# A decoder layer with 32 experts on one core: gate/up weights in 4 MB loads with 32 KB packets, one more early slot, and one piece of a LayerNorm moved from ScalarE and GpSimd to VectorE

## The reference: what is computed

```python
x = LN(alpha * x + hybrid_mixer(x))            # 8 FoX heads + 8 MoBA heads
x = LN(alpha * x + memory_cross_attention(x))  # 4 heads, 256 memory tokens
# moe_ffn: top-4 of 32 experts, softmax over the four
logits = xt @ w_router + b_router
top_val, top_idx = lax.top_k(logits, 4); gates = softmax(top_val)
def expert_block(xb, e):
    h = xb @ w_gate_up[e] + b_gate_up[e]       # 1024 -> 2048
    g, u = min(h[:, :1024], 7), clip(h[:, 1024:], -7, 7)
    return ((u + 1) * g * sigmoid(1.702 * g)) @ w_down[e] + b_down[e]
x = LN(alpha * x + sum_k gates_k * expert_k(x))
```

## Time and profile before

| what | us |
|---|---|
| median of the timed runs | 1237.19 |
| the profiled execution's own time | 1236.11 |
| its span in the trace | 1234.2 |
| PE busy, share of the span | 1156.5, 94% |
| PE's waits for gate/up weights in the experts | 42.7 |
| transfers on SP's queue, share of 16 engines' span | 86.0% |

### The profile page before, as it was taken

How to read it: one execution, slowest core, us unless ns; L and a number is a source line. 1 busy time by engine, 2 the same in 40 slices (tenths; PEclk the granted TensorE clock), 3 DMA queues, 4 the chain that set the end, 5 groups by cost and what they waited for, 6 DMA issues and landing times.

```text
span 1234.2 us, 13113 instructions
## 1 busy us (share of the span) xinstructions
PE 1156.5 (94%) x5364; PEld 524.5 (42%) x5364; DVE 219.2 (18%) x548; ACT 134.6 (11%) x289; POOL 51.2 (4%) x61
## 2 busy tenths in 40 slices
PE   8999999998999999989899999998989898999985
PEld 6686746754344343324233434333333333333321
DVE  1132112114121111111112111211111111111113
ACT  2133101222010000000000000000000000000002
POOL 0033003210000000000000000000000000000000
PEclk9999999998999999999999999999999999999998
DMA  9943333375899999999999999999999999999994
GB/s 357 310 153 136 106 133 136 136 270 193 363 397 429 427 428 430 427 429 429 429 428 427 427 427 427 431 427 429 427 427 430 427 430 428 429 428 427 431 427 184
DMA packets 54349, 445.50 MB, mean 361 GB/s; under 512 B 10120, under 2 KB 11280, under 8 KB 29744
## 3 DMA queue, kind: packets, MB, share of 16 engines
q1 hardware_dynamic: 52160, 440.48, 86.0%
q10 hardware_dynamic: 2160, 4.60, 1.1%
HBM read 444.01 MB, written 1.06 MB: 361 GB/s over the span
## 4 chain that ended last, share of the span: by engine, by line
PE 50%; DMA 46%; DVE 2%; issue 1%; ACT 1%; SPq 0%; POOL 0%; DVEq 0%
DMA ring<-in_w_gate_up 45%; PE bank L1482 18%; PE bank L1164 9%; PE bank L1177 9%; PE bank L1505 6%; PE bank L1389 2%; PE bank L1450 1%; PE bank L1465 1%; PE bank L1334 1%; PE bank L1492 0%; PE bank L1237 0%; PE bank L1312 0%; PE bank L1136 0%; PE bank L1250 0%; DMA x_nat<-in_x 0%
## 5 line engine op out<-in xcount | busy, mean ns | idle before, releaser
L1482 PE MATMUL bank<-ring,PT 128*64 128x512 f32 x2016 | 448.9, 596 | 42.8 <-DMA ring<-in_w_gate_up 42.7
L1482 PEld LDWEIGHTS bank<-ring,PT 128*64 128x64 f32 x2016 | 140.9, 137 | 344.9 <-issue 260.5
L1505 PE MATMUL bank<-ring,NCt 128*64 128x512 f32 x1024 | 229.0, 600 | 0.7 <-ACT NCt L715 0.7
L1505 PEld LDWEIGHTS bank<-ring,NCt 128*64 128x64 f32 x1024 | 71.2, 138 | 155.1 <-issue 142.8
L1164 PE MATMUL bank<-reg_bc,ring 128*128 128x256 f32 x512 | 113.7, 381 | 1.8 <-ACT reg_bc L637 1.8
L1062 DVE TENSOR_SCALAR reg_k<-bank 128x512 f32<-128x512 f32 x32 | 22.1, 692 | 473.1 <-PE bank L1482 473.1
L1164 PEld LDWEIGHTS bank<-reg_bc,ring 128*128 128x128 f32 x512 | 96.3, 190 | 18.1 <-issue 5.4
L706 ACT ACTIVATE reg_v<-reg_k 128x512 f32<-128x512 f32 x32 | 20.2, 630 | 751.1 <-DVE reg_k L1062 751.1
L1079 DVE COPY vc<-bank 128x512 f32<-128x512 f32 x32 | 22.1, 692 | 305.6 <-PE bank L1505 305.6
L1389 PEld LDWEIGHTS bank<-L,reg_a 128*128 128x128 f32 x512 | 64.4, 200 | 24.5 <-issue 23.5
L1389 PE MATMUL bank<-L,reg_a 128*128 128x128 f32 x512 | 70.6, 292 | 0.8 <-DVE L L985 0.8
(11 more groups left out here) (204 smaller groups left out, 494.6 us busy)
## 6 DMA issues: line engine op xcount, KB each, us to landing
ring<-in_w_gate_up SPq DMA_DIRECT2D x126, 2048.0 KB, 24.3
ring<-in_w_down SPq DMA_DIRECT2D x64, 2048.0 KB, 20.3
ring<-in_w_in SPq DMA_DIRECT2D x6, 2048.0 KB, 15.5
ring<-in_w_ck SPq DMA_DIRECT2D x2, 2048.0 KB, 20.6
ring<-in_w_cv SPq DMA_DIRECT2D x2, 2048.0 KB, 10.6
ring<-in_w_mix_out SPq DMA_DIRECT2D x2, 2048.0 KB, 7.7
ring<-in_w_cq SPq DMA_DIRECT2D x2, 2048.0 KB, 7.7
ring<-in_w_co SPq DMA_DIRECT2D x2, 2048.0 KB, 9.5
```

The lines of the kernel that those rows point to most:

```text
L1482: last = mm(ps[half * CAP:(half + 1) * CAP, :], xgT[:, k, i * CAP:(i + 1) * CAP], w[:, j, col:col + HALF], start=False, stop=(k == KD - 1) ...
L1505: last = mm(xy_ps[half * CAP:(half + 1) * CAP, :], hT[:, a:a + CAP], w[:, j, half * HALF:(half + 1) * HALF], start=(k == 0), stop=(k == KD ...
```

## The change

- **Slots.** `kcT` and `vc` (keys and values of the cross-attention) lie in a seventh slot of `ring`, index 6. What else lived in them moves into the freed space of `L`, `reg_v`, `reg_k` and the mask constants; the activation is computed in place. Expert 1 so has three slots (`reg_q`, `reg_bc`, ring 6) that can be filled ahead of the experts.
- **Loads.** For experts 2 to 30 the gate/up weights are two loads of 4 MB (ring 3 and 4, ring 5 and 6); each partition's share is one run of 32 KB on both sides. Experts 0, 1 and 31 keep 2 MB gate/up loads. Down weights keep 2 MB loads, in ring 0 and 1 from expert 2 on. In the steady state ring 2 is idle.
- **Waits.** The first 4 MB load of an expert waits until PE has used the first four steps of the expert before, the second until it has used all eight.
- **LayerNorm.** Tile 1's second half of `x2` goes to DVE (`gain2(1)`, `scale_and_bias2(1)`), behind the places of tile 1.
- **Biases.** The clearing of `bdn` waits for the first expert's gate/up products, and ACT loads it after the first pair; `bgu` is loaded without waiting for a clearing.

```diff
-        ring = sb("ring", [P, CH, SLOT])
+        ring = sb("ring", [P, NSLOT, SLOT])          # CH = 6, NSLOT = 7
-        kcT = sb("kcT", [P, KD, NMEM])
-        vc = sb("vc", [P, 2, D])
+        reg_kv = ring[:, NSLOT - 1, :]
+        kcT = reg_kv[:, 0:2048].rearrange("p (k m) -> p k m", k=KD)
+        vc = reg_kv[:, 2048:4096].rearrange("p (t d) -> p t d", t=2)
...
+        def gate_up_source(e, c, rows=slice(0, GUJ)):                     # GUJ = 4
+            w = w_gate_up[0][bass.ds(e, 1), c * GUJ * P:(c + 1) * GUJ * P, :]
+            return w.rearrange("o (p j) n -> p (o j) n", p=P)[:, rows, :]
+        FIRST = [[ring[:, 0, :], ring[:, 1, :]], [ring[:, 2, :], ring[:, 3, :]]]
+        SECOND = [[early_q, early_bc], [ring[:, 6, :], ring[:, 0, :]]]
+        STEADY = [[ring[:, 3, :], ring[:, 4, :]], [ring[:, 5, :], ring[:, 6, :]]]
+        def gate_up_slots(c):
+            return ring[:, 3 + 2 * c:5 + 2 * c, :].rearrange("p a (j n) -> p (a j) n", j=2)
+        def down_slot(c, e):
+            return ring[:, {0: 4, 1: 1}.get(e, 0) + c, :].rearrange("p (j n) -> p j n", j=DNJ)
...
-            with sp.Fori(3, NE) as n:
-                for c in range(CH):
-                    wait_used(c, n)
-                    load_chunk(n, c)
+            def load_expert(e, n):
+                sp.wait_ge(chunks_used, n * 4 - 2)
+                load_gate_up(e, 0)
+                sp.wait_ge(gu_done, n)
+                load_gate_up(e, 1)
+                sp.wait_ge(chunks_used, n * 4)
+                load_down(e, 0)
+                sp.wait_ge(y_done, n)
+                load_down(e, 1)
+            with sp.Fori(3, NE - 1) as n:
+                load_expert(n, n)
...
-            nc.gpsimd.memset(bdn, 0.0).then_inc(moe_zeroed, 1)
-            for n, (tt, half) in enumerate(((0, 0), (0, 1), (1, 1))):
+            for n, (tt, half) in enumerate(((0, 0), (0, 1))):
...
+            pool.wait_ge(gu_done, 1)
+            nc.gpsimd.memset(bdn, 0.0).then_inc(moe_zeroed, 1)
...
-            normalise(1, 1)
...
             places(S, 0, False, (1,)).then_inc(s_ready, 1)
+            gain2(1)
+            scale_and_bias2(1)
...
-                    if j == 0:
-                        pe.wait_ge(chunk_in[c], n * 16 + 16)
+                    if halves and j == 0:
+                        pe.wait_ge(gate_up_half_in[c], halves * 16)
+                    elif j == (2 if halves else 0):
+                        pe.wait_ge(gate_up_in[c], n * 16 + 16)
```

More of the change, by code:

```diff
@@ L257, in hybrid_layer @@
         hT = NCt[:, :, :].rearrange("p a b -> p (a b)")[:, 0:512]
-        bgu = kcT[:, 0:2, :].rearrange("p k m -> p (k m)")
-        bdn = vc[:, 0, :]
+        bgu = after[:, 1536:2048]
+        bdn = after[:, 0:1024]
         memT = reg_c
@@ L325, in hybrid_layer @@
         moe_zeroed = sem("moe_zeroed")
-        chunk_in = [sem(f"chunk_in{c}") for c in range(CH)]
+        gate_up_in = [sem(f"gate_up_in{c}") for c in range(2)]
+        gate_up_half_in = [sem(f"gate_up_half_in{c}") for c in range(2)]
+        down_in = [sem(f"down_in{c}") for c in range(2)]
         chunks_used = sem("chunks_used")
@@ L455, in _ @@
[L455 to L467, removed]
@@ L468, in _, with load_half @@
-            for c in range(CH):
[L469 to L474, removed]
-            with sp.Fori(3, NE) as n:
-                for c in range(CH):
-                    wait_used(c, n)
-                    load_chunk(n, c)
+            def load_half(e, slot, c, half):
+                done = (gate_up_half_in, gate_up_in)[half][c]
+                sp.dma_start(two_rows(slot), gate_up_source(e, c, HALVES[half])).then_inc(done, 16)
@@ new lines, in _ @@
+            with sp.Fori(3, NE - 1) as n:
+                load_expert(n, n)
+            e = NE - 1
+            for c in range(2):
+                for half in range(2):
+                    if (c, half) == (1, 1):
+                        sp.wait_ge(gu_done, e)
+                    else:
+                        sp.wait_ge(chunks_used, e * 4 - 3 + 2 * c + half)
+                    load_half(e, STEADY[c][half], c, half)
+            sp.wait_ge(chunks_used, e * 4)
+            load_down(e, 0)
@@ L1465, in biases, with gate_up @@
                     mm(ps[:, :], bsel[rows, i, :], bgu[rows, :], start=True, stop=False, skip_group_check=True)
-            def gate_up(p, i, first):
+            def gate_up(p, i, first, halves=0):
                 n = p * 2 + i
@@ L1512, in pair @@
             def pair(p, first=False, with_base=False, last=False):
-                gate_up(p, 0, first)
+                gate_up(p, 0, first, 1 if first else 0)
                 if not first:
@@ L1532, in pair @@
                 down(p, 0, range(KD), first)
-                gate_up(p, 1, first)
+                gate_up(p, 1, first, 2 if first else 3 if last else 0)
                 if not last:
```

159 lines of the change are left out of this document (95 added, 64 removed).

## The result

| kernel | median, us | runs | ratio to before, 95% interval |
|---|---|---|---|
| before | 1237.87 | 4 | |
| changed | 1247.06 | 4 | 1.0073 (1.0054 to 1.0092) |

The change makes the kernel slower by 0.7%. The forecast was 1232.0, faster, in a range from 1228.5 to 1238.5. The profiled execution took 1247.79 us, its span is 1246.0.

The account below looks back on a forecast made before the run. The weight transfers were taken to bound the experts, with PE setting the stream's start. Terms +0.65 - 1.15 - 4.7 = -5.2 gave 1230.9 from the profiled 1236.1, or 1232.0 us against the median 1237.2, range 1228.5 to 1238.5.

Parts of the forecast that it names:

- part 4: Expert loop: waiting for whole 4 MB loads costs 0, at most +1 us, with PE's products the same in number and size.
- pair 6: Experts 12 and 13, with extra PE work: the load of expert 14 just in time, X + 36.25 against X + 36.4.
- part 2: End of the router: x2 work moved from POOL to DVE lets PE's last gather begin sooner, -1.15 us.
- part 1: Slots and waits before expert 3: the early chunk buys only an idle gap, expert 3's data begin later, +0.65 us.
- part 3: Gate/up loads of experts 3 to 30: 32 KB packets make each 4 MB load 0.085 us shorter, -4.7 us in all.
- expert 31's last landing: End of the kernel: halves for expert 31 keep this as the bound, so the 28.3 us after it stay.
- rival B: Start of the experts: shorter DVE waits may keep PE's clock high, 2.9 us earlier in all, 1229.1 us; chance 0.08.
- What B priced as the opposite: Expert loop: PE's clock falls behind each longer wait, 3.9 us a pair, less than the slack of 5.0; no time lost.
- Part 3's line through 2 and 16 KB: Packet cost from two measured stretches: 10.6 ns a packet and 27.2 bytes a ns; 431 to 432 GB/s expected in the experts.
- rival D: Expert loads: a packet's own cost is smaller, 3.5 ns, so part 3 is -1.6 us, total 1235.1; chance 0.10.
- rival A: Expert loads: 32 KB packets are no faster, 16 KB is already the plateau, total 1236.7 us; chance 0.20.
- rival C: Expert loads: the longer runs are read more slowly, +3.7 us at 0.075 a load, up to 1273.7 us; chance 0.10.

Follow-up runs that it names:

- experiment 2: The kernel before, with its gather reading x2 four columns apart instead of two (wrong columns); 1244.99 us, ratio 1.0062.
- experiment 1: The changed kernel, with its gather reading x2 two columns apart instead of four (wrong columns); 1231.43 us, ratio 0.9950.
- experiment 7: The changed kernel's slots, with every gate/up load 2 MB in 16 KB packets with its own wait, and gather distance two; 1230.20 us, ratio 0.9952.
- experiment 5: The kernel before, with the four products of each gather reading x2 every 3rd, 5th, 6th and 8th float (wrong columns); 1240.84 us, timed once.
- experiment 8: The changed kernel, 4 MB loads with 32 KB packets, with x2 stored in pairs so the gather reads every 2nd float and right columns; 1232.26 us, ratio 0.9961.
- experiment 3: The changed kernel, with 4 MB loads as two runs of 16 KB a partition, so gather distance two is right; 1234.85 us, ratio 0.9975.
- experiment 6: The kernel before, with only tile 1's second half of x2 moved to VectorE; 1233.38 us, ratio 0.9966.
- experiment 9: The kernel of experiment 8, with gate/up loads of experts 2, 3, 12 to 15 and 31 in 2 MB halves with a wait each; 1228.51 us, ratio 0.9927.
- experiment 4: The changed kernel, with x2 stored so a gather reads 128 neighbouring floats, LayerNorm 4 apart and the base step 128 apart; 1237.63 us, ratio 0.9998.

## Why the prediction was wrong

**The step that failed** is in part 4: "PE's products are the same in number and size". They are, and it does not follow that they cost the same. I counted `GUJ` as the number of rows in a load and did not follow it into the gather, where it is the distance between the floats that PE reads. So the sum has no term for it. Experiment 2 gives its price on the kernel before, 7.0 us, experiment 1 its price in the changed one, 15.6. Of 57.9 us of PE's work most lies in the waits for weights, but the stream's start is PE's, and the slack of a pair falls from 5.0 to 0.9 us, so that pair 6 breaks the stream for 5.5 us instead of 0 to 1.

The traces show where the larger price in the changed kernel comes from; by their spans it is 14.9 against 8.5 us. Nearly all of the difference is the start: expert 2 is 10.9 us late there and 5.0 in experiment 2. The start loses the high clock that part 2 had won (1.8 us in expert 0's products, where experiment 2's are 0.8 us quicker than before), and the gathers ahead of expert 0 delay its products by 4.8 us instead of 1.7. Another 2.0 us come at the end: with 4 MB hand-overs PE waits for no weights after expert 29's second load, so slow gathers count there, while the kernels of experiments 2 and 7 still wait for their last loads. Pair 6 costs less there than in experiment 2, 1.9 against 3.1.

The Trainium skill ("SBUF — State Buffer", section "Door 1: The DMA port swizzle (why `[64,N]` ≈ `[32,N]`)") names lines of 16 bytes and wants "≥2 hits per line". This rule, which speaks against the change, I had not weighed, and experiments 2, 5 and 8 agree with it: 196 ns with two floats in each 16 bytes, 328 with one. Its next sentence, that 4 fp32 is how far one can stride for free, does not agree: at a distance of 4 the load is slow.

**The other terms,** each from kernels that differ in little else:

| term | forecast | measured | from |
|---|---|---|---|
| parts 1 and 4, slots and 4 MB waits | +0.65 to +1.65 | +1.5 | experiments 3 and 6: 1234.85 - 1233.38 |
| part 2, end of the router | -1.15 | -4.2 | experiment 6: 1233.38 - 1237.58 |
| part 3, 32 KB packets | -4.7 | -3.4, -2.6 | experiments 1 and 8 less 3 |
| the gather's distance | 0 | +15.6 | changed kernel less experiment 1 |

Rows that compare two groups of runs (parts 1 and 4, the -2.6) shift by 0.4 us if each kernel is set against its own runs of before: +1.0 and -2.2.

The size of parts 1 and 4 came out as forecast, though 1.5 is about as large as the intervals, and in part by luck, for it is the difference of two larger numbers. Experiment 7 shows them: handed over in 2 MB the slots are worth 1233.38 - 1230.20 = 3.2 us, and the 4 MB hand-over takes 4.6 back (4.2 each against its own runs of before). The forecast had the reason right, that the early slot buys idle time while expert 3's load waits for half an expert, but not what a shorter wait would give. Nor did expert 31's last landing stay the bound, as part 4 had it: in experiments 1, 3 and 8 PE waits for none of expert 31's weights. Its term for pair 6, 0 to 1 us, was 0.9 in experiment 3 and 2.7 in experiment 1.

Part 2's own term was about right: the gather begins 1.36 us sooner for 1.17. A small price was missed, a wait of 0.24 for the second piece, since the gather's first half took 1.2 us and not 1.9. What was missing is the clock, to which I gave 0.08 as rival B: by the traces 1.1 us in the gather, 1.2 in expert 0's products and 1.3 in its down products. It came in every kernel that has part 2 and the gather's short distance (expert 0's products in 13.95 us in experiments 1, 3, 6, 7, 8 and 9); experiment 4, whose LayerNorm pieces were slower and whose PE waited longer for them (1.18 us ahead of the last gather for 0.73), has 15.46. What B priced as the opposite also came: behind waits of 2.6 us in the loop PE's clock sometimes fell, 8.78 us for 7.09 in the line under experiment 1. Part 3's line through 2 and 16 KB was a little steep: the stretches stand at 429 to 431, not at 431 to 432. The gain of 2.2 to 3.4 lies between it and rival D's 1.6, which these runs do not exclude. Rivals A and C are refuted: 16 KB is not the plateau, and 32 KB is not read more slowly.

Without the failed step the sum would have come out, and partly by luck: experiment 8 has 1232.26 where the forecast was 1232.0, from a larger part 2, a smaller part 3 and a larger sum of parts 1 and 4.

## What to carry to other kernels

When a constant that sets a transfer's layout changes, search every reader of that constant: the distance at which another engine reads its operand can change while counts and shapes stay. In TensorE's weight loads and wide products, and in VectorE's pieces here, it paid to keep at least two float32 in each 16 bytes that were read. And a bound with large waits in the steady state still pays for slower work wherever it leads the stream: at the start and at the one iteration with extra work.

## What was not expected of the hardware

- A 128x128 float32 weight load took 195 ns with its floats side by side, 196 to 200 at every 2nd, 262 at every 3rd, 328 at every 4th, 313 to 335 at every 5th, 6th and 8th.
- The moving side of a product (the operand that is not loaded as weights) has a price too: a read 128 floats apart took 7.14 us for eight records of 512 columns, 3.60 side by side. Distances between were not tried. Writing PSUM two columns of each four cost nothing (3.62 us).
- The price differs by instruction. All kernels here also read `h` 4 floats apart when they transpose it (L1492 before, L1550 changed). Its weight loads took 207 and 220 ns, 140 in the transposes that read neighbours (L1524), and its matmul records 295 ns for 286.
- VectorE's 128x512 `scalar_tensor_tensor` took 1.13 us with its reads 4 floats apart, for 0.74.
- Moving one piece of a LayerNorm from ScalarE and GpSimd to VectorE was worth 4.2 us, of which 2.5 came from the clock that PE kept in the next products (13.95 us for 15.15, 7.09 for 8.43).
